# The first attention's transposes and first two scores inside the last value chunk, and no slab subtraction on GpSimd there

## The reference, cut to what matters

```
def diff_moba_mixer(x, w_in, lam, subln, w_out, lambda_init, rope_d, rope_m):
    h = x @ w_in                       # 256 x 3072: dq, dk, dv, mq, mk, mv, 512 columns each
    ...
    dq, dk = rope(dq), rope(dk)        # 4 heads x 2 maps x 64
    mq, mk = rope(mq), rope(mk)        # 4 heads x 128
    a = diff_attention(dq, dk, dv, lam, subln, lambda_init)   # causal; softmax map 0 - lambda * map 1
    b = moba_attention(mq, mk, mv)     # 256 tokens are one block: causal attention
    return concat([a, b]) @ w_out
```

## Time and profile before

| | us |
|---|---|
| median of three runs | 1401.35 |
| the three runs | 1401.92, 1398.43, 1401.35 |
| profiled execution, own time | 1401.9 |
| its span, first to last instruction | 1400.1 |
| TensorE busy in the span | 1340.8 (96%) |
| VectorE busy | 919.6 (66%) |
| ScalarE busy | 686.4 (49%) |
| GpSimd busy | 115.1 (8%) |
| granted TensorE clock, mean | 0.989 of full |

### The profile page before, as it was taken

The page is one execution under the profiler, slowest core; times in us unless marked ns, Lnnn a source line. Parts: engine busy times, 40 slices in busy tenths (PEclk is TensorE's granted clock), DMA queues, the critical chain, the costliest instruction groups (busy, mean ns, idle before and its releaser), DMA issues.

```text
span 1400.1 us, 18066 instructions
## 1 busy us (share of the span) xinstructions
PE 1340.8 (96%) x7230; PEld 1134.9 (81%) x7240; DVE 919.6 (66%) x1012; ACT 686.4 (49%) x821; POOL 115.1 (8%) x146
## 2 busy tenths in 40 slices
PE   9978999999999999999996999999998999999997
PEld 6857788887987788889874788888887998888886
DVE  4957765656577756656577554787777544687775
ACT  5443444445644444444554443566665443566663
POOL 2021100000321100001013000100001100000000
PEclk9999999999999999999998999999999999999999
DMA  9531555555442655555550052655555441455550
GB/s 346 190 147 54 216 183 190 200 180 181 150 151 92 224 186 204 180 194 196 197 180 1 31 200 86 219 190 193 183 196 195 140 173 61 180 185 203 183 180 30
DMA packets 34771, 233.47 MB, mean 167 GB/s; under 512 B 3993, under 2 KB 4241, under 8 KB 8465
## 3 DMA queue, kind: packets, MB, share of 16 engines
q1 hardware_dynamic: 30080, 217.07, 43.5%
q0 software_dynamic: 4336, 14.77, 3.1%
q10 hardware_dynamic: 288, 0.72, 0.1%
HBM read 231.49 MB, written 1.05 MB: 166 GB/s over the span
## 4 chain that ended last, share of the span: by engine, by line
PE 83%; DVE 9%; ACT 4%; issue 2%; POOL 1%; DMA 1%; DVEq 0%; POOLq 0%; ACTq 0%; SPq 0%
PE ps L1586 17%; PE ps L1580 9%; PE ps L1601 6%; PE ps L1602 6%; PE ps L1603 6%; PE ps L1511 4%; PE ps L1513 4%; PE ps L1512 4%; PE ps L1559 3%; PE ps L1560 3%; PE ps L1564 3%; PE ps L1538 2%; PE ps L1540 2%; PE ps L1539 2%; PE ps L1765 2%
## 5 line engine op out<-in xcount | busy, mean ns | idle before, releaser
L902 DVE TENSOR_TENSOR wl<-raw,wh 128x2048 fp32r<-128x2048 f32 x201 | 459.5, 2291 | 208.2 <-ACT wh L535 207.9
L535 ACT ACTIVATE wh<-raw 128x2048 fp32r<-128x2048 f32 x205 | 390.4, 1908 | 144.1 <-PE ps L1586 77.4
L1586 PE MATMUL ps<-xhl,wh 128*128 128x512 f32 x1216 | 290.1, 391 | 0.0
L1586 PEld LDWEIGHTS ps<-xhl,wh 128*128 128x128 f32 x1216 | 223.5, 188 | 43.2
L1601 PE MATMUL ps<-wh,hh 128*128 128x512 f32 x432 | 169.7, 393 | 5.9 <-DVE hl L1158 4.2
L1602 PE MATMUL ps<-wl,hh 128*128 128x512 f32 x432 | 169.3, 392 | 0.0
L1603 PE MATMUL ps<-wh,hl 128*128 128x512 f32 x432 | 169.0, 391 | 0.0
L1580 PEld LDWEIGHTS ps<-xhl,wl 128*128 128x128 f32 x1216 | 155.8, 191 | 7.3 <-DVE wl L902 1.2
L1580 PE MATMUL ps<-xhl,wl 128*128 128x256 f32 x1216 | 158.6, 283 | 0.8 <-DVE wl L902 0.8
L1511 PE MATMUL ps<-wh,xhl 128*128 128x512 f32 x272 | 107.0, 393 | 2.2 <-DVE xhl L915 2.2
L1513 PE MATMUL ps<-wh,xhl 128*128 128x512 f32 x272 | 105.9, 389 | 0.0
(11 more groups left out here) (220 smaller groups left out, 1795.5 us busy)
## 6 DMA issues: line engine op xcount, KB each, us to landing
raw<-in_w_slabs SPq DMA_DIRECT2D x205, 1024.0 KB, 4.8
qk<-in_mem POOLq DMA_DIRECT2D x2, 1024.0 KB, 5.9
X<-in_x SPq DMA_DIRECT2D x1, 1024.0 KB, 5.6
gains<-in_ln_mix_g POOLq DMA_DIRECT2D x2, 512.0 KB, 5.4
gains<-in_ln_mix_b POOLq DMA_DIRECT2D x2, 512.0 KB, 6.2
gains<-in_ln_ffn_g POOLq DMA_DIRECT2D x2, 512.0 KB, 6.8
gains<-in_ln_ffn_b POOLq DMA_DIRECT2D x2, 512.0 KB, 7.5
gains<-in_mem_norm POOLq DMA_DIRECT2D x2, 512.0 KB, 4.8
```

What stands on the lines that cost most here:

```text
L535: nc.scalar.activation(wh[:, s % RING, :], raw[:, s % LOWS, :], ACT.Copy).then_inc(wh_ready, 1)
L902: nc.vector.tensor_tensor(wl[:, s % LOWS, :], raw[:, s % LOWS, :], wh[:, s % RING, :].bitcast(F32), ALU.subtract)\
L1586: ins = nc.tensor.matmul(ps[bank + a], wa[:, kt, a * P:(a + 1) * P], xhl[:, kt, :, :], start=False, stop=(kt == KT - 1), skip_group_check= ...
```

## The change

TensorE does the convolution weights and fills 0 to 3 ahead of chunk 5, fills 4 to 7 and the scores of pairs 0 and 1 between its halves. Behind chunk 5 it waits for ScalarE's copies of that chunk, since bank 3 is one of those that take the transposed probabilities, and for the fills, and enters the attention with two pairs started. The six matmuls on zeros are left out. ScalarE rounds slabs 13 and 14 between its two pairs of fills, and copies chunk 5 out behind the exponentials of pair 1. VectorE subtracts slab 13 between its fills and slab 14 behind the first `nb`. GpSimd subtracts neither. The wait for all fills gets a name, and the later grouped attention calls it where it had it before.

```diff
@@ GpSimd
-            for j in range(1, LOOKAHEAD):
-                split(st["hy_out"].s0 + j)
             pool.wait_ge(pool_init, 3)
...
@@ ScalarE, softmax(pairs, q0, beside=None, before=None), behind a pair's exponentials
                     ins.then_inc(exp_done, 1)
+                    if before:
+                        before(q - q0)
                     if q > q0:
                         copy_pT(q - 1)
...
-            for c in range(6):
-                splits(g, 2 * c, min(2 * c + 2, 11))
+            def copy_nat(c):
                 copy_a(g, (c, 2 * c), lambda t: nat[:, t, c * CH:(c + 1) * CH])
+
+            for c in range(5):
+                splits(g, 2 * c, 2 * c + 2)
+                copy_nat(c)
...
-            blocks(0, HY_FILLS)
-            splits(g, 11, 12)
+            blocks(0, HY_FILLS, fs=(0, 2))
+            splits(g, 10, 12)
+            blocks(0, HY_FILLS, fs=(4, 6))
...
-            softmax(HY_PAIRS, Q_HY, lambda k: diff_squares(0) if k == 6 else None)
+            softmax(HY_PAIRS, Q_HY, lambda k: diff_squares(0) if k == 6 else None, lambda k: copy_nat(5) if k == 1 else None)
...
@@ VectorE, softmax(pairs, q0, after, first=None), behind a pair's nb
                     ins.then_inc(nb_ready, 1)
+                    if first and q == q0:
+                        first()
                     if q > q0:
                         post(q - 1)
...
-            blocks(0, HY_FILLS)
+            blocks(0, HY_FILLS, fs=(1, 3))
+            splits(g, 10, 11)
+            blocks(0, HY_FILLS, fs=(5, 7))
             dve.wait_ge(lam_exp, 1)
...
-            softmax(HY_PAIRS, Q_HY, beside_hy)
+            softmax(HY_PAIRS, Q_HY, beside_hy, lambda: splits(g, 11, 12))
...
-            dve.wait_ge(wl_ready, st["hy_out"].s0 + LOOKAHEAD)
             splits(st["hy_out"], 0, 1)
...
@@ TensorE: the wait for all fills leaves blocks() and gets a name
+            def blocks_done(base, fills):
+                pe.wait_ge(blk_act, (base + 1) // 2 + (len(fills) + 1) // 2)
+                pe.wait_ge(blk_dve, (base + 1) // 2 + len(fills) // 2)
...
-            def attention(pairs, q0, v):
+            def attention(pairs, q0, v, started=0):
 
                 n = ring(pairs[0][0])
-                for k in range(n - 1):
+                for k in range(started, n - 1):
                     scores(q0 + k, k, *pairs[k])
...
-            for c in range(6):
+            for c in range(5):
                 chunk_a(st["hy_in"], c, 2 * c)
...
-            pe.wait_ge(bank_free, st["hy_in"].f0 + 4 + 9)
-            blocks(0, HY_FILLS, lambda b, t: nat[:, t, b * P:(b + 1) * P], rope_done, lambda f: 2 if f < 4 else 4, warm=6, warm_at=3)
-            attention(HY_PAIRS, Q_HY, nat)
+
+            def hy_blocks(fs):
+                blocks(0, HY_FILLS, lambda b, t: nat[:, t, b * P:(b + 1) * P], rope_done, lambda f: 2 if f < 4 else 4, warm_at=None, fs=fs)
+
+            def first_scores(half):
+                if half == 0:
+                    hy_blocks(range(4, 8))
+                    pe.wait_ge(bank_free, st["hy_in"].f0 + 4 + 10)
+                    for k in range(2):
+                        scores(Q_HY + k, k, *HY_PAIRS[k])
+
+            hy_blocks(range(4))
+            chunk_a(st["hy_in"], 5, 10, between=first_scores)
+            pe.wait_ge(bank_free, st["hy_in"].f0 + 4 + 12)
+            blocks_done(0, HY_FILLS)
+            attention(HY_PAIRS, Q_HY, nat, started=2)
...
             qk_blocks(range(2, 6), warm=12)
+            blocks_done(8, QK_FILLS)
             attention(QK_PAIRS, Q_QK, nat)
```

More of the change, by code:

```diff
@@ L590, in blocks, with softmax @@
                     ins.then_inc(blk_act, 1)
-            def softmax(pairs, q0, beside=None):
+            def softmax(pairs, q0, beside=None, before=None):
                 def copy_pT(q):
@@ L1030, in blocks, with softmax @@
                     ins.then_inc(blk_dve, 1)
-            def softmax(pairs, q0, after):
+            def softmax(pairs, q0, after, first=None):
                 def post(q):
@@ L1697, in blocks @@
                     ins.then_inc(blk_T, 1)
-                if fs[-1] == len(fills) - 1:
-                    pe.wait_ge(blk_act, ea + (len(fills) + 1) // 2)
-                    pe.wait_ge(blk_dve, ea + len(fills) // 2)
             def scores(q, bank, kind, t, j):
```

## The result

The changed kernel takes 1392.61 us (median of 5 runs, 1391.66 to 1393.57); the kernel before took 1401.92 in the runs beside it (1398.43 to 1406.24). The ratio is 0.9932, 95% interval 0.991 to 0.9953, that is 9.5 us less (6.6 to 12.6), where 7.8 less and a time of 1393.6 were forecast. The profiled execution took 1392.61, its span 1390.8, its mean clock 0.992.

What follows compares the result with a forecast made beforehand. Bound: TensorE's 5.00 us wait on an `nb` held by GpSimd, then a low clock. First transpose 6.75 plus pace 1.05 gives 7.8 off 1401.35: 1393.6 us, range 1391.5 to 1396, taken out to 1390.5.

Steps and rivals of the forecast that it cites:

- What bounded the kernel: First attention: one VectorE `nb` held 3.56 us by GpSimd's subtraction, TensorE waiting 5.00 us before the first transpose of probabilities.
- Rival B: First attention: the long `nb` belongs to the first pair, not to GpSimd; 1396.4 us, chance 0.05.
- TensorE up to the second half: Around chunk 5: convolution weights and fills hidden without waits, first half 71.1 to 76.6, second 79.7 to 85.15 us.
- The added wait: Behind chunk 5: TensorE waits for ScalarE's copy out of bank 3, 0.9 us, until 86.05; ScalarE has 0.7 to spare.
- The first transpose: First transpose of probabilities in the first attention at 86.6 instead of 93.35, 6.75 us earlier.
- The pace: First attention's pairs: at full clock VectorE binds at 1.45 instead of 1.77 us apart; 1.05 us gained.
- What moves behind: Behind the first attention: later slab loads and the second attention's waits cost 0, the lead stays.
- rival D: Later stages: the lead is given back at a fixed wait, such as a late slab; 1399 to 1401 us, chance 0.06.
- The clock: First attention: granted clock 1.00 throughout, where it had been 0.66 from 93.30 to 102.40 us.
- rival A: First attention: the clock falls anyway and the pace part is lost; 1394.9 us, chance 0.12.
- rival C: Clock falls behind chunk 5, low until the output projection's first tile is done; its matmuls 8.3 us; 1410.4, chance 0.04.
- the wait's upper bound: Pause behind chunk 5: 2.5 us if ScalarE comes late by a slab, 1.6 more; range's upper end 1396.

Runs made afterwards that it cites:

- run 1: The kernel before with only the GpSimd part: VectorE subtracts slabs 13 and 14, TensorE's order untouched; 1398.0 us, 0.9971 of the kernel before.
- run 2: As run 1, plus five matmuls on zeros ahead of the first and two ahead of the second transposes of probabilities; 1396.15 us, one run.
- run 4: The changed kernel with GpSimd subtracting slabs 13 and 14 again, VectorE neither; 1393.79 us, 0.9943 of the kernel before.
- run 6: The changed kernel with two unread ScalarE copies of 1024 elements ahead of its copies of chunk 5; 1395.7 us, one run.
- run 5: The changed kernel with the first two scores behind chunk 5, ScalarE's copy and VectorE's slab 14 ahead of the softmax; 1395.02 us, 0.9949 of before.
- run 3: The kernel before with 22 unread matmuls on zeros ahead of the first transpose of probabilities; 1401.01 us, 0.9994 of the kernel before.
- run 7: The changed kernel with GpSimd's two slab subtractions in the second, grouped attention moved to VectorE; 1382.18 us, 0.9867 of the kernel before.
- run 8: As run 7, with the two banks of transposed probabilities exchanged in the first attention; 1381.38 us, 0.9857 of the kernel before.

## Why the prediction was right

Point by point, by its own steps.

- **What bounded the kernel.** Right. One `nb` was held by GpSimd's subtraction: it is normal without it (runs 1 and 2) and long again with it (run 4), whichever order TensorE has. Rival B is out.
- **TensorE up to the second half.** The order and each hiding place came out as said; the sizes were too large in sum. I had the halves start at 71.1 and 79.7 and the second end at 85.15; they started at 70.79 and 79.00, and the last matmul of the second starts at 84.42, so at the chunk's pace of 0.23 the next could have started at 84.65. I had taken row durations of whole groups (1.91 for 16 transposes) and added 0.1 for each switch, though a row's end overlaps the next row's start: ahead of the chunk 16 transposes stand 1.72 from their first start to the next matmul's (69.07 to 70.79). The pieces ahead of the first half and between the two were 0.77 too large; the halves themselves took 5.57 and 5.65, together 0.27 more than forecast, and hid some of it. The net is the 0.5 by which this part fell short.
- **The added wait.** 0.9 forecast for copy and signals, idle 0.69 by the row, or 0.84 from 84.65 to 85.49. ScalarE's spare time was forecast as 0.7 and is 0.99. The price beyond it held in run 4, one for one, and was wrong in run 6, nearly three for one, where the clock fell.
- **The first transpose.** 6.75 earlier forecast; 7.30 measured, 7.37 from chunk 4's end. Of the 0.55, 0.50 is the term above, and 0.05 the wait with pair 2's scores (1.40 against 1.45).
- **The pace.** 1.05 forecast, 1.03 measured (8.40 less 7.37). VectorE binds, at 1.37 rather than 1.45: the same overlap of rows, which the step from pair 3 to 4, 1.35 instead of 1.3, gives back in part. That the two agree within 0.02 is in part luck: the prediction's own steps end at a lead of 7.7, which is 0.95 over 6.75, and the sum took 1.05 without a source for the other 0.1.
- **What moves behind.** Right: the lead was 8.33 on every step of GpSimd's from 96.75 to 320.75. It swung later and was never given back, so rival D did not come.
- **The clock.** The forecast held at 1.00, and A and C did not come. But my argument against A, that a clock once full stays so with pauses like these, leant on the stretch from 102.40 to 117.00, and runs 1, 5 and 6 show the clock falling after pauses of 0.5 to 1.8 in this very place. With 0.69 and 0.91 it did not, nor with 1.33 and 0.90 (run 4). I had also put 0.5 of idle in each pair; it was 0.27. So the forecast came true, but its reason was not enough.
- **The time.** 7.8 forecast, about 9.5 by the ratio (6.6 to 12.6). The traces account for 8.40 here; the rest lies within the interval, and the two profiled executions differ by low-clock stretches elsewhere. Two small slips of the working change nothing: rival C's 8.3 is 8.2 by its own numbers, and the wait's upper bound gives 1395.2, not 1396.

## What to carry to other kernels

Where a tiny VectorE instruction takes microseconds in a trace, look for a GpSimd instruction that ends with it; find all places of the pattern, since here the untouched one was worth more than the changed one (9.53 against 8.40 us in the traces). Work taken off GpSimd is best put where VectorE idles beside dense matmuls, and a wait is cured either by removing what makes it long or by placing it beside such matmuls: measure the two alone before adding them up. Price a longer TensorE pause twice, by its length and with what the low clock would do to the work behind it, since the runs here show both; and add up start-to-start distances, not durations.

## What the runs showed of the hardware that I had not expected

The clock fell after sequences of short pauses: 0.60, 0.88, 1.44 and 0.50 us (run 1), 1.45 and 0.50 (run 5), 1.77 and 0.90 (run 6). It stayed up with 0.69 and 0.91 (the changed kernel), but also with 1.33 and 0.90 (run 4), which add up to more than run 5's. Every kernel here also has pauses of about 0.94, 0.58, 0.79 and 1.42 in its later pairs at a clock of 1.00. So the length of the pauses doesn't settle it alone; what else does is not shown. Filled with matmuls on zeros, the stretch of run 1 stayed at 1.00 (run 2), and so did that of the old kernel's long pause (run 3). A fall cost 0.8 and 1.4 us by these two comparisons, and some 0.4 (run 5) and 2.0 (run 6) by what is left of the stretch when the longer waits are taken off. The page that I had set aside for rival A, the Trainium skill's "TensorE: Matmul & The Clock Gate", section "A second HAM failure mode: psum-queue depth-cycling", tells of short idles between groups of matmuls that make the clock swing; runs 1, 5 and 6 agree with it, at 0.50 after pauses all under 2 us, and run 4 does not show it.

It also falls at places that differ from one execution to the next. The kernel before, then the changed one, in stages that the change leaves alone:

```profile
345.00:350.00 5.00, 5.00 (x26) 4.25 (x26) 0.69 (x1) 4.92 (x7) 0.00 (x0) 0.66 0.15 57
```

```profile
425.00:430.00 5.00, 4.02 (x11) 3.19 (x12) 4.83 (x6) 0.59 (x2) 1.20 (x2) 0.66 0.02 3
```

TensorE is busy 5.00 of 5.00 us in the first of these, and had no pause over 0.4 us in the 12 us ahead of it. Ahead of the second it had pauses of 1.67 and 1.07, and the kernel before, with the same two, kept its clock there. The lead of the changed kernel goes from 8.33 to 9.86 across the first and back to 8.21 across the second, with nothing changed in either stage. Such stretches, 1.5 to 1.7 us each, come in one execution and not in the next (those of runs 7 and 8 have neither), so a few of them could make up the scatter of single runs (1398.43 to 1406.24); that they are its cause was not tested.

A small VectorE instruction can be held for all of what is left of GpSimd's: two elements per partition 3.73 and 3.95 us, 16 elements 4.46. Held were `tensor_scalar`s and a `tensor_tensor` with both inputs in SBUF (3.79). Not held beside GpSimd's subtraction were the maxima from PSUM (0.42; 0.41 in run 4), and a `tensor_scalar` of one element per partition (0.15 at 79.61 in run 4, where GpSimd's second subtraction runs from 79.45 to 84.05). The Trainium skill ("SBUF — State Buffer", section "Who interferes with whom") names the two held kinds and the maxima in the same way, and the trace agrees with each. GpSimd took 4.50 to 4.60 for the slab that VectorE subtracts in 2.29.

The hold seems to go the other way too. In run 7 two of GpSimd's `rstd` steps, which take 0.20 and 1.64 us in the changed kernel's trace, took 0.76 and 3.55 beside VectorE's two slab subtractions. It cost nothing there: GpSimd's lead over the changed kernel is 1.79 us ahead of these steps and 1.78 behind them.
